# A mixture-of-experts encoder layer: the first block's token rows chosen on chip, and four smaller moves in queues and order

## Chip, cores, metric

One core of one Trainium2 chip. The metric is the device time of one execution in microseconds; the time before is the median of 3 runs.

## What is computed

All in float32, on 768 tokens of 1024 features (a prompt of 256 and a sample of 512). The two sequences meet nowhere but share all weights.

```python
h = rmsnorm(x, attn_norm)
c_q, c_kv, k_pe, dq, dk, dv = split(h @ w_in)
x = x + concat(mla(c_q, c_kv, k_pe), diff_attention(dq, dk, dv)) @ w_out
t = rmsnorm(x, ffn_norm)
g = argmax(softmax(t @ router_group + bias))                      # one of 4 groups
w2, e2 = top_k(softmax((t @ router_expert + bias)[group g]), 2)   # two of its 8 experts
out = sum over the two experts e of gate_e * (silu(t @ w_gate[e]) * (t @ w_up[e])) @ w_down[e]
y = rmsnorm(x + out, final_norm)
```

There are 32 experts with 256 inner columns: 1 MB each for gate, up and down, 3.15 MB an expert. 768 tokens make 1536 (token, expert) pairs.

## The kernel before

**Stages.** Projection and attention fill the first 388 us. Then six tiles of 128 tokens go through the out projection and the routing (388 to 486 us), then 32 experts one after another (to 775), then the combination of pairs with the residual and the last norm.

**Routing.** For each tile t VectorE adds the residual (`residual`, L1165), evacuates half of the transposed tile (L1170), computes `h2 = x * rs * gain` in one instruction (`ffn_norm`, L1176, written with the features reordered), picks group and two experts (`route`, L1193), and places the pairs in the experts' slots (`place`, L1229): TensorE's `rank` (L1608) counts the pairs of the same expert in earlier tokens, two one-hot matrices say which slot modulo 64 a token takes, and TensorE's `place` (L1622) sums, over the tiles, a table of token and pair ids for the first 64 slots of every expert. `slots` (L1247) gives the full slot number of each pair. ScalarE computes squares and root of the norm and evacuates the other half of the transposed tile. GpSimd stores h2 to HBM (L699) and scatters the pair numbers to a table of slots in HBM (`note_pairs`, L690): two scatters a tile.

**Experts.** An expert's pairs come in blocks of 64. The first block of each takes its token ids from the table in PSUM (`ids_main`); further blocks take them from the table in HBM, which the sync queue loads once (L557) and VectorE shifts into ids (`ids_further`, L1297). GpSimd gathers the rows of h2 by ids (`gather`, L713), four experts ahead, TensorE transposes them (`rows_transpose`, L1657), VectorE copies the result to `x_eT` (L1349). Gate/up is one group of 16 matmuls with the tokens stationary (`gate_up`, L1664), two 64-column halves of the array side by side; SiLU on ScalarE (L972), product on VectorE (L1326), a transpose of h (L1709), its copy (L1331), four matmuls for down (`down`, L1675), a copy by ScalarE (L980), a scatter to HBM by GpSimd (L725). 40 blocks in all, 8 of them further ones.

**Order.** All is written out by hand with semaphores, and each engine takes its instructions in program order. TensorE's order in block s is gate/up of s, transposes of the rows of s+1, down of s-1, transpose of h of s (`pe_group`, L1716). VectorE's is product of s, (ids_further, in the first block only,) copy of rows of s+1, copy of h of s (`dve_group`, L1338). The counts, which say how many further blocks an expert has, come from a chain of small VectorE instructions (L1279 to L1295) that follows the last placement; TensorE, ScalarE and GpSimd wait for them ahead of the first block.

**Weights.** Six slots for experts. The sync queue (SP) loads experts 0 to 3 at 389 us, 4 and 5 once the out projection is over (the slots hold its operands), expert 31 into the place of x, and each later expert e once the down product of e-6 is done (`load_expert`, L515, with `sp.wait_ge(last_done, e - RING + 1)`, L530); each third of an expert also waits for the third before the last issued one (L526). Between 5 and 31 that queue has

```python
store_residual(NT - 1)
sp.wait_ge(ids_scattered, 2 * NT * 16)
for h in range(2):
    sp.dma_start(yids_sb[h * SLOTS:(h + 1) * SLOTS, NE:]..., ids_dram...).then_inc(ids_loaded, 16)
sp.wait_ge(x2_stored, NT * 16)
...
load_expert(NGRP - 1, members(NGRP - 1)[-1])
```

## Time and profile before

| | us |
|---|---|
| median of 3 runs (lowest, highest) | 811.07 (810.74, 811.63) |
| the profiled execution's own time | 813.74 |
| its span, first to last instruction | 812.0 |
| TensorE busy (matmuls) | 714.7, 88% |
| VectorE, ScalarE, GpSimd busy | 322.1, 214.0, 200.9 |
| mean granted TensorE clock | 0.955 of full |
| bytes moved by DMA | 154.64 MB, mean 190 GB/s |

Times in the rows are microseconds from the start of the span. In a timeline a row has start, length, engine, line, operation, output and inputs, the count of merged instructions, and in brackets how long the engine sat idle before and what ended that. Matmuls in float32 are two instructions each; a transpose is one. In a row of windows each engine has its busy time and instruction count (TensorE's matmuls, its weight loads, VectorE, ScalarE, GpSimd), then come TensorE's granted clock, the busy share of the 16 DMA engines and GB/s. In a row of DMA queues stand packets, MB and share; q1 is the sync queue's, q0 GpSimd's. In a row of waits stand the total in us, how many, and the longest.

### The profile page before, as it was taken

The numbers are of one execution on the slowest core, as the hardware profiler recorded it, in microseconds if no ns is written. First come the engines' busy times: TensorE is split into PE (matmuls) and PEld (weight loads), VectorE is DVE, ScalarE is ACT, GpSimd is POOL, SyncE is SP. The second block draws the span as 40 slices with busy tenths as digits, with TensorE's granted clock in tenths as the row PEclk, the third lists the DMA queues.
The fourth block names the chain that finished last, engine by engine and source line by source line (L and its number), as shares of the span: only waits on it lengthen the run. The fifth ranks groups of instructions, "written<-read, shape, count | busy, mean of one in ns | idle before, by whom it ended". The sixth has DMA issues, their size and how long they took to land. (4 is left out here: it accounts for less than half of the span.)

```text
span 812.0 us, 12300 instructions
## 1 busy us (share of the span) xinstructions
PE 714.7 (88%) x3978; PEld 404.9 (50%) x3979; DVE 322.1 (40%) x900; ACT 214.0 (26%) x575; POOL 200.9 (25%) x478
## 2 busy tenths in 40 slices
PE   6899999999898999998999974999987999998810
PEld 3455544444365666664455552555544555554500
DVE  3853121110078988881545562111211221111138
ACT  2433211011167777772211110111110111110122
POOL 1224231220014230232001123441332433541110
PEclk9999999999979999999999986999999999999975
DMA  8703002000140000000792158899999999999856
GB/s 302 292 1 105 0 1 103 1 0 1 39 174 1 1 2 1 1 2 1 293 417 120 67 206 304 289 348 372 371 352 388 368 376 361 379 363 377 361 221 257
DMA packets 40824, 154.64 MB, mean 190 GB/s; under 512 B 9642, under 2 KB 10794, under 8 KB 31936
## 3 DMA queue, kind: packets, MB, share of 16 engines
q1 hardware_dynamic: 33120, 138.20, 45.5%
q0 software_dynamic: 7648, 15.75, 5.8%
q8 instruction: 28, 0.46, 0.2%
q14 instruction: 28, 0.23, 0.1%
HBM read 142.29 MB, written 20.03 MB: 200 GB/s over the span
## 5 line engine op out<-in xcount | busy, mean ns | idle before, releaser
L1405 PE MATMUL banks<-arena 128*128 128x512 f32 (+1 forms) x384 | 163.2, 579 | 9.9 <-DMA arena<-w_in 7.6
L1670 PE MATMUL banks<-arena 128*64 128x256 f32 x1280 | 151.2, 390 | 11.5 <-DMA arena<-w_up 7.4
L1670 PEld LDWEIGHTS banks<-arena 128*64 128x64 f32 x1280 | 95.0, 140 | 60.9 <-issue 18.6
L1405 PEld LDWEIGHTS banks<-arena 128*128 128x128 f32 x384 | 72.1, 193 | 85.2 <-issue 78.0
L1561 PE MATMUL banks<-arena 128*128 128x512 f32 x192 | 86.4, 598 | 1.1 <-DVE arena L1162 1.1
L1679 PE MATMUL banks<-arena 128*64 128x512 f32 x320 | 79.7, 610 | 0.5 <-ACT arena L980 0.5
L1326 DVE TENSOR_TENSOR arena<-arena,banks 128x128 f32<-128x128 f32 x40 | 11.5, 287 | 165.7 <-ACT arena L972 165.7
L1118 DVE TENSOR_REDUCE arena<-banks 128x1 f32<-128x512 f32 (+1 forms) x96 | 55.2, 598 | 52.0 <-PE banks L1477 43.9
L903 ACT ACTIVATE arena<-banks,arena 128x512 f32<-128x512 f32 (+1 forms) x96 | 58.2, 611 | 45.7 <-DVE arena L1121 22.3
L1561 PEld LDWEIGHTS banks<-arena 128*128 128x128 f32 x192 | 35.1, 190 | 38.8 <-issue 37.5
L972 ACT ACTIVATE arena<-banks 128x128 f32<-128x128 f32 x40 | 11.1, 277 | 161.3 <-PE banks L1670 161.3
L725 POOL DMA_INDIRECT pair_rows<-arena x40 | 40.4, 1010 | 35.2 <-POOL arena L723 33.1
L717 POOL DMA_INDIRECT arena<-h_rows,arena x40 | 39.1, 977 | 34.9 <-POOL arena L715 34.9
L836 ACT ACTIVATE arena<-banks,arena 128x512 f32<-128x512 f32 (+1 forms) x24 | 16.0, 666 | 113.8 <-PE banks L1405 112.8
L1512 PE MATMUL banks<-arena 128*128 128x128 f32 x240 | 36.8, 285 | 8.5 <-issue 6.4
L1477 PE MATMUL banks<-arena 96*128 96x512 f32 (+1 forms) x96 | 41.9, 562 | 2.1 <-ACT arena L903 1.2
L1660 PE MATMUL banks<-arena 64*128 64x64 f32 x320 | 28.8, 231 | 15.7 <-DMA arena<-h_rows,arena 15.7
L1512 PEld LDWEIGHTS banks<-arena 128*128 128x128 f32 x240 | 26.7, 144 | 31.0 <-issue 26.5
L463 POOL TENSOR_SCALAR arena<-arena 128x2 f32<-128x2 f32 (+1 forms) x8 | 1.5, 193 | 154.4 <-ACT arena L931 154.4
L607 POOL TENSOR_TENSOR arena<-arena 128x64 f32<-128x64 f32 (+2 forms) x24 | 7.9, 327 | 124.6 <-ACT arena L836 69.9
L980 ACT ACTIVATE arena<-banks 128x512 f32<-128x512 f32 x32 | 19.1, 597 | 71.8 <-PE banks L1679 71.8
L1660 PEld LDWEIGHTS banks<-arena 64*128 64x128 f32 x320 | 23.3, 141 | 28.9 <-issue 17.8
(179 smaller groups left out, 856.3 us busy)
## 6 DMA issues: line engine op xcount, KB each, us to landing
arena<-w_gate SPq DMA_DIRECT2D x32, 1024.0 KB, 12.8
arena<-w_up SPq DMA_DIRECT2D x32, 1024.0 KB, 13.4
arena<-w_down SPq DMA_DIRECT2D x32, 1024.0 KB, 13.1
arena<-w_in SPq DMA_DIRECT2D x3, 2048.0 KB, 8.4
arena<-pair_rows SPq DMA_DIRECT2D x5, 1024.0 KB, 11.2
arena<-w_out SPq DMA_DIRECT2D x1, 4096.0 KB, 12.9
arena<-xT SPq DMA_DIRECT2D x6, 512.0 KB, 10.3
arena<-x SPq DMA_DIRECT2D x6, 512.0 KB, 10.7
```

The lines of the kernel that those rows point to most:

```text
L717: pool.indirect_dma_start(x_rows[i], None, h2_dram, bass.IndirectOffsetOnAxis(ap=id_cur[0:SLOTS, i:i + 1], axis=0), bounds_check=T - 1, oo ...
L725: pool.indirect_dma_start(y_dram, bass.IndirectOffsetOnAxis(ap=yid_cur[:, i:i + 1], axis=0), y_sb[i], None, bounds_check=4 * T - 1, oob_is ...
L903: act.activation(p_tok[u % 3][:, a, 0:nt * P], bank(2 * (u % 2) + a)[:, 0:nt * P], ACT.Exp, bias=nbias[:, u % 4, a:a + 1], scale=MLA_SCALE ...
L980: act.activation(y_sb[s % YBUF], bank(4), ACT.Copy).then_inc(y_out, 1)
L1118: dve.reduce_max(mx[:, u % 4, a:a + 1], bank(2 * (u % 2) + a)[:, 0:nt * P], X_).then_inc(dve_chain, 1)
L1405: last = nc.tensor.matmul(bank(mm % 2)[:, 0:GROUP_COLS[g]], xgT[:, t, c, :], w[:, c, :], start=(c == 0), stop=(c == DC - 1))
L1477: nc.tensor.matmul(bank(2 * (u % 2) + a)[:, 0:nt * P], qT[0:QK, 2 * j + a, tok], kT[0:QK, 2 * j + a, keys], start=True, stop=True).then_in ...
L1512: last = nc.tensor.transpose(bank(4 + tau % 2)[:, kt * P:(kt + 1) * P], p_tok[u % 3][:, a, kt * P:(kt + 1) * P], ident)
L1561: last = nc.tensor.matmul(bank(2 * (t % 2) + h), aT[:, c, t * P:(t + 1) * P], w_out_sb[:, c, h * 512:(h + 1) * 512], start=(c == 0), stop= ...
L1660: last = nc.tensor.transpose(bank(b)[:, c * SLOTS:(c + 1) * SLOTS], x_rows[i][:, c * P:(c + 1) * P], ident[half, half])
L1670: last = nc.tensor.matmul(bank(b)[h * SLOTS:(h + 1) * SLOTS, 0:2 * P].rearrange("p (g n) -> p g n", g=2), x_eT[i][:, c, :], w[:, :, c, h * ...
L1679: last = nc.tensor.matmul(bank(4)[h * SLOTS:(h + 1) * SLOTS, :], h_T[:, j * SLOTS:(j + 1) * SLOTS], w[:, j, h * 512:(h + 1) * 512], start= ...
```

## The change

- h2 loses its gain: ScalarE writes `x * rs`, VectorE computes only the reciprocal. The gain is multiplied in where VectorE took the transposed rows out of PSUM (all 40 blocks), from a new 4 KB column load; the 512 KB broadcast of gain goes.
- The rows of expert 0's block are not gathered: VectorE weighs the one-hot slot matrices with the mask of expert 0 and the norm (`choose`), TensorE multiplies them with x, six tiles summed in bank 4 (`choose`, the two halves of the features in the two halves of the columns), ScalarE copies the sum, 16 matmuls transpose it.
- The sync queue stores the last residual tile ahead of the weights of experts 4 and 5. Before expert 31 it waits no longer for the scatters of ids; it waits for the last selection instead.
- The table of further ids is loaded on ScalarE's queue, after the first SiLU. VectorE's `ids_further` moves behind the copies of the first block.
- VectorE's count chain moves behind the multiply for expert 0; TensorE waits for the counts after the first gate/up. The first down product comes ahead of the second gate/up.
- On chip memory is laid out anew for this; the counts move from bank 1 to bank 2.

```diff
@@ sync queue
+                    sp.dma_start(gain_rows, A["ffn_norm"].rearrange("o (p c) -> (o p) c", c=DC)).then_inc(lam_loaded, 16)
...
-            sp.dma_start(gain_ffn, A["ffn_norm"].to_broadcast([P, D])).then_inc(gffn_in, 16)
...
             sp.wait_ge(oproj, 2 * NT)
+            store_residual(NT - 1)
             load_expert(0, 4)
             load_expert(0, 5)
-            store_residual(NT - 1)
-            sp.wait_ge(ids_scattered, 2 * NT * 16)
-            for h in range(2):
-                sp.dma_start(yids_sb[h * SLOTS:(h + 1) * SLOTS, NE:].rearrange("r (b e) -> r b e", e=NE),
-                             ids_dram.rearrange("(b r e) o -> r b (e o)", b=NBLK, e=NE)[:, 1:, :]).then_inc(ids_loaded, 16)
             sp.wait_ge(x2_stored, NT * 16)
             sp.wait_ge(h2_ready, NT)
             sp.wait_ge(rms2_ready, NT)
             sp.wait_ge(x2T_psum, 2 * NT)
+            sp.wait_ge(chosen_psum, 1)
             load_expert(NGRP - 1, members(NGRP - 1)[-1])
@@ GpSimd
-            gather_main(0, 0)
+            pool.sem_inc(id_ready, 1)
             gather_main(0, 1)
             note_pairs(NT - 1)
@@ ScalarE
+            def ffn_norm(t):
+
+                act.wait_ge(norm_ready, t + 1)
+                if t >= 2:
+                    act.wait_ge(h2_stored[t % 2], 16 * (t // 2))
+                act.activation(h2[t % 2].rearrange("n (c p) -> n c p", c=DC), x_tok[:, t, :].rearrange("n (p c) -> n c p", c=DC),
+                               ACT.Copy, scale=rs[:, t:t + 1]).then_inc(h2_ready, 1)
...
+            act.wait_ge(chosen_psum, 1)
+            act.activation(x_sel, bank(4), ACT.Copy).then_inc(chosen_rows, 1)
             act.wait_ge(gates_in, 1)
             act.activation(gate_in, gate_in, ACT.Exp).then_inc(gates_exp, 1)
...
+            def load_further_ids():
+
+                act.wait_ge(ids_scattered, 2 * NT * 16)
+                for h in range(2):
+                    act.dma_start(yids_sb[h * SLOTS:(h + 1) * SLOTS, NE:].rearrange("r (b e) -> r b e", e=NE),
+                                  ids_dram.rearrange("(b r e) o -> r b (e o)", b=NBLK, e=NE)[:, 1:, :]).then_inc(ids_loaded, 16)
...
                     silu(e + before)
+                    if isinstance(g, int) and e == 0:
+                        load_further_ids()
@@ VectorE
+            def choose(t):
+
+                for i, mask in enumerate((m1_all, m2_all)):
+                    dve.tensor_scalar(share[:, i:i + 1], mask[:, t, 0:1], rs[:, t:t + 1], None, ALU.mult).then_inc(dve_chain, 1)
+                    chain[0] += 1
+                dve.wait_ge(dve_chain, chain[0])
+                dve.wait_ge(onehot_ready, 2 * t + 2)
+                link(dve.tensor_scalar(select[:, t, :], onehot[:, 0, 0:SLOTS], share[:, 0:1], None, ALU.mult))
+                dve.scalar_tensor_tensor(select[:, t, :], onehot[:, 1, 0:SLOTS], share[:, 1:2], select[:, t, :],
+                                         ALU.mult, ALU.add).then_inc(select_ready, 1)
...
             slots(NT - 1)
+            dve.wait_ge(xeT_psum, 1)
+            dve.tensor_tensor(x_eT[0], bank(0).rearrange("p (c n) -> p c n", c=DC), gain_eT, ALU.mult).then_inc(xeT_ready, 1)
 
             dve.wait_ge(counts_psum, 1)
...
                     h_product(k)
+                    if not isinstance(g, int) or e + 1 < NE:
+                        dve.wait_ge(xeT_psum, e + 2)
+                        dve.tensor_tensor(x_eT[(s + 1) % 2], bank(0).rearrange("p (c n) -> p c n", c=DC), gain_eT, ALU.mult).then_inc(xeT_ready, 1)
+                    hT_evac(k)
                     if isinstance(g, int) and e == 0:
                         ids_further()
-                    if not isinstance(g, int) or e + 1 < NE:
-                        dve.wait_ge(xeT_psum, e + 2)
-                        dve.tensor_copy(x_eT[(s + 1) % 2], bank(0).rearrange("p (c n) -> p c n", c=DC)).then_inc(xeT_ready, 1)
-                    hT_evac(k)
@@ TensorE
+            def choose(t):
+
+                pe.wait_ge(select_ready, t + 1)
+                for h in range(2):
+                    last = nc.tensor.matmul(bank(4)[h * SLOTS:(h + 1) * SLOTS, :], select[:, t, :],
+                                            x_tok[:, t, h * 512:(h + 1) * 512], start=(t == 0), stop=(t == NT - 1))
+                return last
...
             router(NT - 1, 1)
+            for t in range(3):
+                choose(t)
             rank(NT - 1)
+            choose(3)
+            place(NT - 1)
+            choose(4)
+            choose(5).then_inc(chosen_psum, 1)
...
-            place(NT - 1)
...
+                    early = first and s == 1
...
+                    if early:
+                        down_weights(g, 0)
+                        down_before(k, g, 0, last_done)
                     pe.wait_ge(xeT_ready, e + 1)
                     gate_up(1, s % 2, weights(g, s)).then_inc(gu_done, 1)
                     if not isinstance(g, int) or e + 1 < NE:
                         transpose_rows(g, s + 1)
-                    if not isinstance(g, int) or e:
+                    if first and s == 0:
+                        pe.wait_ge(counts_ready, 1)
+                        words = load_counts(pe, g)
...
+                    elif not early:
                         down_weights(g, s - 1)
                         down_before(k, g, s - 1, last_done)
...
-            pe.wait_ge(rows_in[0], 16)
-            rows_transpose(0, 0, range(DC)).then_inc(xeT_psum, 1)
-            pe.wait_ge(counts_ready, 1)
+            pe.wait_ge(chosen_rows, 1)
+            x_sel_c = x_sel.rearrange("n (p c) -> n c p", c=DC)
+            for c in range(DC):
+                for h in range(2):
+                    half = slice(h * SLOTS, (h + 1) * SLOTS)
+                    last = nc.tensor.matmul(bank(0)[half, c * SLOTS:(c + 1) * SLOTS], x_sel_c[half, c, :], ident[half, half],
+                                            start=True, stop=True)
+            last.then_inc(xeT_psum, 1)
             pe_group(0)
```

## Rows read from the trace of the kernel before

**Rows 1.** Windows: us, busy us by engine, clock, DMA share, GB/s.

```profile
476.50:496.50 20.00, 6.05 (x36) 5.53 (x35) 10.52 (x45) 2.60 (x6) 8.48 (x11) 0.57 0.99 382
496.50:500.50 4.00, 2.69 (x16) 2.04 (x18) 0.86 (x3) 0.29 (x2) 2.23 (x5) 0.50 0.25 47
500.50:510.50 10.00, 8.91 (x69) 5.89 (x66) 1.73 (x5) 1.56 (x3) 1.72 (x4) 0.87 1.01 333
510.50:514.50 4.00, 4.00 (x31) 2.00 (x32) 1.27 (x3) 0.81 (x2) 2.30 (x4) 1.00 0.45 112
600.00:640.00 40.00, 34.58 (x259) 18.94 (x257) 7.04 (x16) 4.37 (x10) 11.32 (x20) 0.96 1.02 373
```

**Rows 2.** Timeline of TensorE: start us, us, instruction, idle before.

```profile
476.84 2.03 PE L1603 MATMUL banks<-arena 128*128 128x36 f32 x16
...
485.50 1.09 PE L1627 MATMUL banks<-arena 128*128 128x64 f32 x4
496.93 1.11 PE L1660 MATMUL banks<-arena 64*128 64x64 f32 x8 [10.34 <-DMA arena<-h_rows,arena]
498.92 5.75 PE L1670 MATMUL banks<-arena 128*64 128x256 f32 x32 [0.88 <-DVE arena L1358]
...
506.73 3.67 PE L1670 MATMUL banks<-arena 128*64 128x256 f32 x32 [1.05 <-DVE arena L1349]
...
510.98 1.94 PE L1679 MATMUL banks<-arena 128*64 128x512 f32 x8
...
513.10 3.67 PE L1670 MATMUL banks<-arena 128*64 128x256 f32 x32
```

**Rows 3.** Timeline of the sync queue (SP).

```profile
498.07 1.32 SPq L557 DMA_DIRECT2D arena<-pair_of_slot  x2
...
513.36 0.35 SPq L534 DMA_DIRECT2D arena<-w_gate  x1
...
519.64 0.33 SPq L534 DMA_DIRECT2D arena<-w_gate  x1
```

**Rows 4.** Waits of TensorE from 513, and of SP from 470.

```profile
PE banks L1670 <- DMA arena<-w_up: 7.4, 5, 2.5
...
SPq L531 <- PE banks L1679: 20.6, 5, 11.7
```

**Rows 5.** Timeline of VectorE.

```profile
475.61 0.69 DVE L1168 TENSOR_TENSOR arena<-arena,banks 128x512 f32<-128x512 f32 x1 [1.48 <-PE banks L1561]
477.04 0.69 DVE L1174 COPY arena<-banks 128x512 f32<-128x512 f32 x1 [0.75 <-PE banks L1592]
...
478.12 2.06 DVE L1184 SCALAR_TENSOR_TENSOR arena<-arena 128x1024 f32<-128x1024 f32 x1
...
487.43 0.18 DVE L1279 COPY arena<-banks 1x32 f32<-1x32 f32 x1
...
489.95 0.16 DVE L1294 CAST arena<-arena 1x12 int32<-1x12 f32 x1
...
505.01 0.29 DVE L1326 TENSOR_TENSOR arena<-arena,banks 128x128 f32<-128x128 f32 x1 [6.07 <-ACT arena L972]
...
505.58 0.40 DVE L1304 TENSOR_SCALAR arena<-arena 128x352 uint32<-128x352 uint32 x1
```

**Rows 6.** Timeline of ScalarE.

```profile
498.97 0.23 ACT L964 ACTIVATE arena<-arena 128x30 f32<-128x30 f32 x1 [19.79 <-DVE arena L1311]
500.44 1.28 ACT L972 ACT_TABLE_LOAD   x1 [1.23 <-issue]
```

**Rows 7.** DMA queues: two from 488.6 to 490.6, q1 from 499.9 to 501.

```profile
q1 hardware_dynamic: 113, 0.79, 94.1%
q0 software_dynamic: 105, 0.03, 6.6%
...
q1 hardware_dynamic: 1123, 0.16, 99.7%
```

**Rows 8.** DMA queue q1 from 514 to 528.5.

```profile
q1 hardware_dynamic: 644, 3.83, 79.1%
```

More of the change, by code:

```diff
@@ L222, in build @@
         gain_in = k.take(DC)
+        gain_rows = k.take(DC)
         gains = k.take(4)
@@ L275, in build @@
         macc = m.take(NT * NE).rearrange("p (t e) -> p t e", t=NT)
-        bias_r = m.take(NG + NE)
-        ones = m.take(P)
-        logit = m.take(NT * (NG + NE)).rearrange("p (t e) -> p t e", t=NT)
-        top = m.take(1)
-        max_g, max_1, max_2 = (m.take(NT) for _ in range(3))
-        rank_f = m.take(2)
-        onehot = m.take(2 * P).rearrange("p (i n) -> p i n", i=2)
-        slot_of = m.take(4 * NE).rearrange("p (i w e) -> p i w e", i=2, w=2)
         r_g = m.take(3 * NG)
@@ L286, in build @@
         slot_f = m.take(2)
-        junk_c = m.take(256).bitcast(bf16)
+        rank_f = m.take(2)
+        bias_r = m.take(NG + NE)
+        top = m.take(1)
+        max_g, max_1, max_2 = (m.take(NT) for _ in range(3))
+        share = m.take(2)
         cnt = m.take(NE)
@@ L291, in build @@
         pk = m.take(NGRP * RING)
+        logit = m.take(NT * (NG + NE)).rearrange("p (t e) -> p t e", t=NT)
         m = Area(WORDS - DC * (NG + NE) - DC, WORDS)
@@ L1261, in _ @@
                 x2T_evac(t)
-                ffn_norm(t)
+                norm(t)
                 route(t)
@@ L1355, in dve_group @@
                             hT_evac(k + j + 1)
-            dve.wait_ge(xeT_psum, 1)
-            dve.tensor_copy(x_eT[0], bank(0).rearrange("p (c n) -> p c n", c=DC)).then_inc(xeT_ready, 1)
             gate_inputs()
@@ L1648, in _ @@
             router(NT - 1, 1)
+            for t in range(3):
+                choose(t)
             rank(NT - 1)
-            counts = bank(1)[:, 0:NE]
+            choose(3)
+            place(NT - 1)
+            choose(4)
+            choose(5).then_inc(chosen_psum, 1)
+            counts = bank(2)[:, 0:NE]
             nc.tensor.matmul(counts, ones, macc[:, NT - 2, :], start=True, stop=False)
@@ L1716, in pe_group @@
             def pe_group(g):
-                words = load_counts(pe, g)
+                first = isinstance(g, int) and g == 0
+                if not first:
+                    words = load_counts(pe, g)
                 for s in members(g):
                     e = g * RING + s
-                    n, before = extras(words, s)
-                    k = e + before
                     if is_last(g, s):
@@ L1726, in pe_group @@
                         pe.wait_ge(up_loaded[s], 16 * (g + 1))
+                    early = first and s == 1
+                    if not first or s:
+                        n, before = extras(words, s)
+                        k = e + before
+                    if early:
+                        down_weights(g, 0)
+                        down_before(k, g, 0, last_done)
                     pe.wait_ge(xeT_ready, e + 1)
```

41 lines of the change are left out of this document (24 added, 17 removed).

## Prediction, made before the changed kernel was run

> **What bounds the kernel now.** I read the stretch totals first, then each engine in order of time, then who waited for whom. [Rows 1] cut the switch from routing to experts into stretches. From 476.5 to 496.5 the DMA engines are full (share 0.99) with the weights of experts 4 and 5. Then they are nearly empty to 500.5 (0.25), full while expert 31 loads, half empty from 510.5 to 514.5 (0.45), and full again until the last weights (1.02 in the row of 600 to 640, 373 GB/s). TensorE's granted clock is 0.57 and then 0.50, its lower level of 1.2 GHz. [Rows 2] show why: its last routing work starts at 485.50, the gathered rows of expert 0 let it go on at 496.93 after 10.3 idle us, the first gate/up product starts at 498.92, the second at 506.73, and the first down product at 510.98. [Rows 3] show the sync queue behind that: it waits until 498.07 for the scatters of ids, loads the ids, issues expert 31 only then, and expert 6 at 513.36, after that down product; expert 7 follows at 519.64, behind the down product of expert 1. Later TensorE loses only 7.4 us to weights, in five waits of at most 2.5 [rows 4]. The sync queue waits for down products five times, 20.6 us in total, the first 11.7 [rows 4]. So from 514 on the weight stream, 25 experts long, sets the end, and TensorE has a few us of slack. What counts is how much sooner the stream runs without holes.
>
> **The change, part by part.** *Normalization.* The fused norm and gain leaves VectorE (2.06 us, starting 478.12) and a scaled copy goes to ScalarE. For tiles 0 to 4 both lie beside the out projection, which keeps TensorE back to back. In the last tile the logits are done at 476.84 + 2.03 = 478.87, so routing starts at 478.95 and not at the norm's end, 478.12 + 2.06, about 480.1 [rows 2, 5]: 1.1 us earlier. The selection weights add four small VectorE operations a tile, under 1 us, less than what leaves: nothing. The multiply by gain that takes the place of a 128x512 copy reads a bank as the residual add of that shape does, 0.69 us, and so long is the copy too [rows 5]: nothing.
>
> *Selection.* A down product is 4 matmuls in 1.94 us [rows 2] with the same shapes as two selections, so one selection is 0.97 us. Three fit where TensorE idles now, and so does the fourth. The last placement would start at 485.5 - 1.1 = 484.4, takes 0.56, and two more selections follow: 486.9. ScalarE copies (0.60), then 16 matmuls transpose. In instructions that is 32, each between 0.069 us (8 transposes in 1.11 at half clock, halved) and 0.127 (16 logit instructions in 2.03) [rows 2]: 2.2 to 4.1 us; I take 3.4, nearer to the logits, whose instructions also load new weights each time. VectorE adds 0.69, the start 0.15. The first gate/up starts at 491.7, not 498.92: 7.2 us earlier.
>
> *First block.* The count chain, 2.7 us [rows 5], now stands behind the first gain multiply: counts at 494.3. ScalarE then needs 2.75 us from the gate exponential to the end of its table load [rows 6], so SiLU is done near 497.6 and the product at 497.9, later than gate/up itself. Rows of expert 1 are the first gather of GpSimd's queue, issued where expert 0's was, which let TensorE go on at 496.93 [rows 2], so they come about 497 to 498, and their transposed copy is ready at 499.4. The first down product is now ahead of the second gate/up: 499.7 to 501.7. The second gate/up starts at 501.7 (5.0 earlier), and expert 6 is issued at 502 instead of 513.36.
>
> *Weight stream.* Expert 31 is issued near 487, when 4 and 5 still occupy the engines. The holes go: 4.0 x 0.75 + 4.0 x 0.55 = 5.2 us. The last residual store ahead of the weights delays them: that add ends at 475.61 + 0.69 = 476.30 [rows 5], where today the weights go as soon as TensorE is through, near 475.5, and the store's issue comes on top in part: 0.9. One gather less is about 0.15 MB, 0.4 us. Without any new stall the stream is 5.2 - 0.9 + 0.4 = 4.7 us earlier. At the start of the kernel one more small load stands ahead of the third tile's x in the sync queue. An issue there takes up to 0.66 us (two in 1.32 [rows 3]); hidden if the first tiles' work covers it, passed on in full if not: 0 to 0.66, I take 0.4 later. The 512 KB broadcast of gain that goes was hidden in a stretch where experts 0 to 3 load long before use: nothing.
>
> *The ids of further blocks, now on ScalarE's queue.* This decides. They are two loads of 704 runs of 128 bytes. 1123 packets of the sync queue move 0.16 MB in 1.1 us [rows 7], so each run is a packet: 88 for each of 16 engines. Today they go when that queue holds nothing else, and VectorE finds them landed right behind its first product, at 505.3 [rows 5]. In the change they go near 499 (the scatters of ids stand behind the gather in GpSimd's queue, and ScalarE first does SiLU), while the sync queue holds expert 31 and then 6. How two queues share an engine is in [rows 7]: between 488.6 and 490.6 GpSimd's queue has 105 packets for 0.03 MB, the sync queue 113 for 0.79 MB. They alternate one for one, whatever the size. That is 113/16 = 7.1 turns in 2 us, 0.283 us a turn; 88 turns need 25 us. No row has a load on ScalarE's queue; the nearest are GpSimd's.
> The Trainium skill says otherwise for the size of a turn (DMA: Bandwidth & Descriptors, section Queues, rings and completion order): an engine drains a whole packet, typically 9 to 17 descriptors, before it switches. By that, 88 descriptors are 5 to 10 turns, some 3 us, and the 4.7 us would be kept; it is a rival below.
>
> By the rows, the sync queue has work until: 476.5 + 0.9 + 20 - 0.4 = 497.0, expert 31 with gathers 9.0, expert 6 with gathers 9.5, so 515.5. Until then 15.7/0.283 = 55 of 88 turns are done; the rest run alone in 1 us: landed at 516.5. VectorE waits for them **ahead of expert 1's product**, which would be ready at 505.7. Behind it stand the copy of expert 2's rows, TensorE's transpose of h, gate/up of expert 2, and the down product of expert 1, for which the sync queue waits before expert 7. VectorE needs 0.7 for the ids (505.3 to 505.98) and 0.29 for the product [rows 5], then the copy: gate/up of expert 2 starts at 518.6, not 513.10 [rows 2]. After 12 idle us TensorE is at half clock, as it was for the product at 498.92: 5.75 us instead of 3.67 [rows 2], 2.1 more. Transposes (1.11 at half clock, halved) and the down product of expert 1 take 0.6 + 1.94 more, to 526.9, and expert 7 is issued at 527.3 instead of 519.64, its data from 528.6.
> The stream has then nothing from 515.5 to 528.6. Today the sync queue moves 3.83 MB from 514 to 528.5 [rows 8]; expert 6 is 3.15 of them, so 0.68 MB of expert 7 and about one gather and one scatter (0.35) are ahead of the new kernel: 1.03/0.368 = **2.8 us later**. TensorE is 7.6 us later at expert 2, but its five waits for weights, 7.4 us [rows 4], absorb that, so the stream sets the end: +2.8, +0.4 at the start = **+3.2**. On the profiled execution: span 812.0 to 815.2. That execution took 813.74, the median of the runs is 811.07, 2.7 less, and I carry the difference over: 814.3.
>
> **Rivals.** (a) *The ids land in time.* If a turn takes many small packets, or ScalarE's loads share the sync queue's order, or the sync queue runs dry before expert 6 is issued (that needs the first down product 3.5 us later than I have it, and then 1 us empties the ids), VectorE's wait is 0 to 2 us. For: the product at 505.7 has 6 us after their issue, and today, issued from 498.07 on, they are there by 505.3 at the latest. Against: the one-for-one rows. Time: 811.07 - 4.7 + 0.4 = 806.8. The point from which it decides is ids landed at 505.
> (b) *A draw.* The stall is there, but the ids end sooner (turns against 4 KB packets are shorter) or the half clock is avoided: then expert 7 comes 3 us earlier, its lag of 2.8 is gone: 811.5.
> (c) *TensorE carries its delay to the end.* At most one wait, 2.5 us of the 7.6, is absorbed, because the sync queue then waits for slots and the stream slips with TensorE: 811.07 + 5.1 + 0.4 = 816.6. For: five waits for down products exist already. Against: only the first is long.
> (d) *The rows chosen on chip don't come early*, because ScalarE or the gather of expert 1 holds the second block at 506 as now: then the first block moves nothing, but the stream still gains its holes: 807 to 809 if the ids are in time.
>
> **How the numbers follow.** Forecast 814.3, chance 0.62. Rival (a) 0.23, (d) 0.03, (b) 0.07, (c) 0.05. About 0.2% (1.6 us) is what can be told from no change here. The forecast's own range is 812.0 to 816.5, of which a tenth lies within 0.2%. Faster: 0.23 + 0.03 and a little: 0.27. Same: 0.07 + 0.06 = 0.13. Slower: 0.60. The range must reach to (a) and lean to (c): 806.3 to 817.0. Its middle is unlikely; the two cases stand apart.
>
> **What would show it.** Right: two loads of pair_of_slot by ScalarE of 12 us or more to landing; VectorE's shift of ids starting near 516; TensorE idle some 12 us before gate/up of expert 2, at half clock behind; DMA share near 0 from 516 to 528; the first gate/up near 491.7 and expert 6's issue near 502. Wrong: ids shifted before 508 with expert 2's gate/up near 506 and no hole in the DMA row; then the time is below 808. If the hole is there and the time is still lower, my count of the stream is wrong.

## The result: 0.9% slower, and the profile after

The changed kernel took 819.76 us (median of 4 runs, 816.40 to 821.52) beside 811.35 us for the kernel before (4 runs, 810.74 to 812.97): ratio 1.0091, 95% interval [1.0067, 1.0115]. (The ratios here are estimates from all runs; the quotient of these two medians is 1.0104.) It is slower, as forecast, but by 8.4 us and not by 3.2, and 819.76 lies outside the range of 806.3 to 817.0. The profiled execution took 816.40 (span 814.6), the fastest of the four.

In that execution the last router product starts at 474.26 and not at 476.84 [rows 2]. The edit touches little ahead of it, and in the other profiles below that date lies anywhere from 473.70 to 478.91. So two kernels are compared by the time since that product ("since the logits"), and only differences of that are read. The timeline of TensorE in the changed kernel (start, duration, line and form, idle time before it and what ended it):

```profile
474.26 2.03 PE L1633 MATMUL banks<-arena 128*128 128x36 f32 x16
...
484.83 2.14 PE L1809 MATMUL banks<-arena 64*64 64x64 f32 x32
487.92 6.65 PE L1713 MATMUL banks<-arena 128*64 128x256 f32 x32 [0.95 <-DVE arena L1308]
...
497.40 3.72 PE L1722 MATMUL banks<-arena 128*64 128x512 f32 x8 [0.59 <-DVE arena L1363]
500.83 3.74 PE L1713 MATMUL banks<-arena 128*64 128x256 f32 x32
...
516.84 0.48 PE L1752 MATMUL banks<-arena 128*128 128x128 f32 x1 [11.63 <-DVE arena L1358]
517.53 5.51 PE L1713 MATMUL banks<-arena 128*64 128x256 f32 x32 [0.21 <-DVE arena L1379]
```

The first half is the plan of the change, and it works: first gate/up at 487.92, second at 500.83, with the down product of expert 0 ahead of it. Then TensorE is idle for 11.63 us on VectorE, and gate/up of expert 2 starts at the lower clock: 5.51 us instead of 3.67. Since the logits it starts at 43.27, in the kernel before at 36.26 [rows 2]: 7.0 later. VectorE, the queue of ScalarE and the sync queue of the same kernel say why:

```profile
515.70 0.34 DVE L1333 TENSOR_SCALAR arena<-arena 64x352 uint32<-64x352 uint32 x1 [18.56 <-DMA arena<-pair_of_slot]
516.07 0.40 DVE L1336 TENSOR_SCALAR arena<-arena 128x352 uint32<-128x352 uint32 x1
516.50 0.29 DVE L1358 TENSOR_TENSOR arena<-arena,banks 128x128 f32<-128x128 f32 x1
```
```profile
496.51 1.36 ACTq L1008 DMA_DIRECT2D arena<-pair_of_slot  x2
```
```profile
484.22 0.33 SPq L540 DMA_DIRECT2D arena<-w_gate  x1
...
501.56 0.35 SPq L540 DMA_DIRECT2D arena<-w_gate  x1
...
525.89 0.33 SPq L540 DMA_DIRECT2D arena<-w_gate  x1
```

The ids are issued at 496.51 and are not there until 515.7, 19 us later; in the kernel before, VectorE shifted them right behind its first product of 505.01, without a wait [rows 5]. Expert 31 is issued at 484.22, expert 6 at 501.56 and expert 7 at 525.89: since the logits, 6 is 9.2 us earlier than in the kernel before and 7 is 8.8 later [rows 3]. How the ids travelled is read from the DMA queues (packets, MB, share; q1 is the sync queue, q10 ScalarE's). Of their 1440 packets, 1408 of them runs of 128 bytes, none starts in the 4.9 us behind the issue. First the stretch from 501.4 to 504, then that from 504 to 506:

```profile
q1 hardware_dynamic: 222, 0.93, 92.2%
q10 hardware_dynamic: 224, 0.03, 7.5%
```
```profile
q1 hardware_dynamic: 94, 0.39, 75.5%
q10 hardware_dynamic: 952, 0.12, 52.6%
```

In the first the two queues take turns one for one: 14 turns on each of the 16 DMA engines in 2.6 us, 0.19 us a turn. In the second the sync queue has little to move, between the weights of expert 31 and those of expert 6, and two thirds of the ids pass. The other 264 packets need until 515.2, beside the weights of expert 6, and VectorE waits for the last of them. By windows, the DMA engines fall empty at 514 (the columns are the window, its length, busy time of PE, PEld, DVE, ACT and POOL, granted clock, DMA share, GB/s):

```profile
508.00:512.00 4.00, 0.00 (x0) 0.00 (x0) 0.00 (x0) 0.00 (x0) 0.00 (x0) 0.50 1.01 401
...
514.00:516.00 2.00, 0.00 (x0) 0.00 (x0) 0.30 (x1) 0.00 (x0) 0.00 (x0) 0.50 0.10 32
516.00:518.00 2.00, 0.95 (x4) 0.52 (x6) 1.59 (x5) 0.00 (x0) 0.00 (x0) 0.50 0.00 0
...
520.00:526.00 6.00, 6.00 (x41) 3.12 (x39) 1.13 (x3) 0.68 (x2) 3.06 (x7) 0.89 0.26 72
```

How far behind is the stream? The DMA queues from the logits to 52 us behind them, first the kernel before (476.84 to 528.84), then the changed one (474.26 to 526.26); q0 is GpSimd's:

```profile
q1 hardware_dynamic: 3906, 13.96, 74.3%
q0 software_dynamic: 1217, 2.23, 13.7%
```
```profile
q1 hardware_dynamic: 2384, 13.11, 69.0%
q0 software_dynamic: 808, 1.37, 8.5%
q10 hardware_dynamic: 1440, 0.18, 2.8%
```

With the 0.18 MB of ids counted in, the sync queue's work is 0.67 MB behind, where the forecast had 0.68. GpSimd's is 0.86 MB behind, where it had 0.35. GpSimd's row of that stretch says why: it waits for the same shifted ids ahead of all its further gathers, those of main rows too, and stands still for 23.16 us.

```profile
518.28 0.18 POOL L718 COPY arena<-arena 64x1 uint32<-64x1 uint32 x1 [23.16 <-issue]
```

Later, who waited for whom in the changed kernel, TensorE's rows from 510 on, and then the sync queue's from 470 on; against [rows 4] the waits for weights fell from 7.4 to 3.6 us, and the sync queue's waits for down products rose from 20.6 (5 times) to 66.5 (10 times):

```profile
PE banks L1703 <- DMA arena<-h_rows,arena: 5.0, 3, 3.8
PE banks L1713 <- DMA arena<-w_up: 3.6, 3, 1.6
```
```profile
SPq L537 <- PE banks L1722: 66.5, 10, 22.1
```

### The profile page after: what moved, and what is told of

Read it like the earlier page. It is cut to its first block and busy times, and to the rows that moved or that the text cites. A ratio compares the mean times of both kernels' runs of the same rounds, so it can differ in the third digit from the quotient of the medians.

```text
span 814.6 us, 12425 instructions
## 1 busy us (share of the span) xinstructions
PE 721.7 (89%) x4026; PEld 406.1 (50%) x4027; DVE 315.0 (39%) x918; ACT 227.3 (28%) x582; POOL 199.7 (25%) x476
## 3 DMA queue, kind: packets, MB, share of 16 engines
q10 hardware_dynamic: 1440, 0.18, 0.2%
## 5 line engine op out<-in xcount | busy, mean ns | idle before, releaser
L1713 PE MATMUL banks<-arena 128*64 128x256 f32 x1280 | 153.2, 394 | 8.2 <-DMA arena<-w_up 3.6
L1713 PEld LDWEIGHTS banks<-arena 128*64 128x64 f32 x1280 | 96.0, 142 | 59.7 <-issue 17.4
L1722 PE MATMUL banks<-arena 128*64 128x512 f32 x320 | 81.5, 621 | 1.1 <-DVE arena L1363 0.6
L1591 PEld LDWEIGHTS banks<-arena 128*128 128x128 f32 x192 | 35.1, 190 | 38.8 <-issue 37.5
L1507 PE MATMUL banks<-arena 96*128 96x512 f32 (+1 forms) x96 | 40.0, 539 | 2.1 <-ACT arena L906 1.2
L1121 DVE COPY arena<-banks 128x512 f32<-128x512 f32 x12 | 8.3, 689 | 65.3 <-PE banks L1481 65.3
L1722 PEld LDWEIGHTS banks<-arena 128*64 128x64 f32 x320 | 20.8, 139 | 23.6 <-issue 18.4
## 6 DMA issues: line engine op xcount, KB each, us to landing
arena<-w_up SPq DMA_DIRECT2D x32, 1024.0 KB, 12.8
arena<-w_down SPq DMA_DIRECT2D x32, 1024.0 KB, 13.7
```

The costliest lines, as they stand in the source:

```text
L1507: nc.tensor.matmul(bank(2 * (u % 2) + a)[:, 0:nt * P], qT[0:QK, 2 * j + a, tok], kT[0:QK, 2 * j + a, keys], start=True, stop=True).then_in ...
L1591: last = nc.tensor.matmul(bank(2 * (t % 2) + h), aT[:, c, t * P:(t + 1) * P], w_out_sb[:, c, h * 512:(h + 1) * 512], start=(c == 0), stop= ...
L1713: last = nc.tensor.matmul(bank(b)[h * SLOTS:(h + 1) * SLOTS, 0:2 * P].rearrange("p (g n) -> p g n", g=2), x_eT[i][:, c, :], w[:, :, c, h * ...
L1722: last = nc.tensor.matmul(bank(4)[h * SLOTS:(h + 1) * SLOTS, :], h_T[:, j * SLOTS:(j + 1) * SLOTS], w[:, j, h * 512:(h + 1) * 512], start= ...
```

## The experiments

Each kernel was run 4 to 12 times and is set against the kernel before, run on the same chip beside it. They came in four groups, with medians of the kernel before of 812.87 (the first four kernels), 812.75 (the next four), 812.34 (the next four) and 812.48 us (the last two). TensorE computes 40 blocks of rows, expert by expert: a main block each, and eight further ones at experts 8, 9, 13 (three), 14, 15 and 19.

**The changed kernel again** (no edit).

> The changed kernel once more, for a second trace and the spread of its times. Theory (ids on ScalarE's queue take one turn each against weights, VectorE, GpSimd and TensorE wait behind them): VectorE's shift of ids again near 515 to 518, a hole of 11 to 14 us in the DMA engines, 6 to 10 us slower than before in the median. Rival (the loss is in this one execution, or lies elsewhere): the ids land at another time, and the time moves with something else.

819.18 us (816.84 to 821.59), ratio 1.0076 [1.0057, 1.0094]. Since the logits, gate/up of expert 2 starts at 43.30, as in the first trace (43.27), and the ids are shifted at 41.5 (41.4); the wait for them is 18.9 us. But they travelled otherwise: 474 of their packets had started by 510, 31.1 since the logits, where the first trace had 1176 by 31.7, and the rest went on in turns to the end (99 packets of each queue from 510 to 512, 0.32 us a turn, with 7.5 KB in a packet of weights). So the same date was reached in two ways.

**The ids back on the sync queue, behind expert 31:**

```diff
             load_expert(NGRP - 1, members(NGRP - 1)[-1])
+            sp.wait_ge(ids_scattered, 2 * NT * 16)
+            for h in range(2):
+                sp.dma_start(yids_sb[...], ids_dram...).then_inc(ids_loaded, 16)
...
                     silu(e + before)
-                    if isinstance(g, int) and e == 0:
-                        load_further_ids()
```

> Only the two loads of ids go back to the sync queue, now behind expert 31's weights and ahead of expert 6's. Theory: in one queue they need no turns, they land behind expert 31, near 504 to 507, VectorE waits 0 to 2 us, the hole in the DMA engines is gone, and the kernel is 3.5 to 5.5 us faster than before (about 806 to 808). Rival (the loss is the chosen rows, the early down product or the store ahead of the weights): the time stays above 815.

812.74 us, ratio 1.0003 [0.9988, 1.0018]: the loss is gone, the 3.5 to 5.5 us of gain that I expected are not there. In one queue the ids stand behind the weights of expert 31 and take no turns with those of expert 6: shifted 12.8 us after their issue and not 19.2, but VectorE still waits 12.0 us, where I expected 0 to 2.

**ScalarE's queue, but only blocks 1 to 3 of 11** (24 runs of 128 bytes an engine and not 88; enough for these inputs, where no expert has more than three further blocks):

```diff
-  act.dma_start(yids_sb[..., NE:]..., ids_dram...[:, 1:, :])
+  act.dma_start(yids_sb[..., NE:4 * NE]..., ids_dram...[:, 1:4, :])
```

> Still on ScalarE's queue, but only the ids of further blocks 1 to 3 of 11: 24 runs of 128 bytes for each DMA engine, not 88 (no expert of this input has more blocks; the rest of the table is not loaded). Theory, one turn a run at 0.28 us: 6.8 us to landing plus 1 to 2, so VectorE's shift near 505 to 507 and the time at or below before's, 805 to 809. Rival, a turn takes 9 to 17 runs: then 88 runs would be 5 to 10 turns and 24 runs 2 to 3, both few us, and the landing hardly changes with the number. Rival, the wait is for the scatters of ids: the shift stays near 515.

811.08 us, ratio 0.9981 [0.9965, 0.9997]: shifted 12.1 us after issue, VectorE waits 11.3. The first packet starts 4.8 us after the issue, which the expected 8 to 9 us left out. Since the logits, the third gate/up starts at 36.8 with the ids on the sync queue and at 36.1 with three blocks, beside 43.3 in the changed kernel and 36.3 in the kernel before. So the loss of the change hangs on the landing of the ids, and that, on ScalarE's queue, on the number of their runs.

**GpSimd waits for the ids only where it gathers a further block:**

```diff
-            pool.wait_ge(ids_ready, 3)
+            pool.wait_ge(ids_ready, 2)
...
                     with pool.If(n > 0):
+                        pool.wait_ge(ids_ready, 3)
                         await_count(e_xeT_psum, before + 1)
```

> The changed kernel, but GpSimd waits for the shifted ids only where an expert has a further block, no longer ahead of the gather of expert 4. Theory (what my sum left out: GpSimd's gathers of experts 4 to 7 and the first scatter stood behind the ids as well and came on top of the weights later): gathers 4 to 6 are issued before 505, the hole in the DMA engines is as long, and the time is 1.5 to 2.5 us below the changed kernel's. Rival (TensorE's delay alone sets the loss): no difference beyond 0.5 us.

821.58 us, ratio 1.0109 [1.0086, 1.0132], where I expected 1.5 to 2.5 us less than the changed kernel's: the gathers now take turns as well, and the ids land still later (VectorE of this kernel):

```profile
522.77 0.34 DVE L1334 TENSOR_SCALAR arena<-arena 64x352 uint32<-64x352 uint32 x1 [23.69 <-DMA arena<-pair_of_slot]
```

So letting GpSimd go on in those 23 us won nothing: what its gathers gained, the ids lost.

At this point I held that TensorE's date is the bound up to expert 15 and that a delay of it is passed on in full but for the one wait of 1.75 us ahead of expert 13. The next runs were made to test that, and it fell.

**The kernel before, with more work for TensorE alone:** the gate/up products of experts 3 and 4 computed twice.

```diff
+                    if isinstance(g, int) and g == 0 and s in (3, 4):
+                        gate_up(1, s % 2, weights(g, s))
                     gate_up(1, s % 2, weights(g, s)).then_inc(gu_done, 1)
```

> The kernel before, in which TensorE computes the gate/up product of expert 3 and of expert 4 twice (two times 3.67 us more, the same values written again), and nothing else is touched. These products stand behind the issue of expert 7 and well ahead of the one wait for weights before expert 13 (1.75 us). Theory of the forecast (the weight stream sets the end, TensorE's five waits for weights absorb 7.4 us): no change, ratio 0.998 to 1.002. Theory now (TensorE carries a delay through to the expert at which the slots are full, where the load of expert 21 waits for the last product of expert 15, and only the wait of 1.75 us before expert 13 is absorbed): +5.6 us, ratio 1.0069, with expert 21 issued 5 to 6 us later against the last logits and in a burst of three loads.

813.95 us, ratio 1.0016 [0.9996, 1.0036]: 1.2 us for 7.3 us of work, and the interval still includes no change. The +5.6 us of my theory is refuted; "no change", by the theory of the forecast, is nearly right here. At expert 16 TensorE is 6.9 us late all the same, so the rest goes later, at expert 27. TensorE of the kernel before waits there for weights and then starts a product at the lower clock (2.53 + 5.36 - 3.67 = 4.2 us lost); with the extra work it does neither (first the kernel before, then this one):

```profile
737.50 5.36 PE L1670 MATMUL banks<-arena 128*64 128x256 f32 x32 [2.53 <-DMA arena<-w_up]
```
```profile
738.82 3.67 PE L1670 MATMUL banks<-arena 128*64 128x256 f32 x32
```

**The ids on ScalarE's queue, VectorE shifts them at expert 3 and not at expert 0** (right only where the first further block comes later, as here; GpSimd's wait as above):

```diff
-                    if isinstance(g, int) and e == 0:
+                    if isinstance(g, int) and e == 3:
                         ids_further()
```

> The changed kernel with its ids on ScalarE's queue, but VectorE shifts them only at expert 3, and GpSimd waits for them only where it gathers a further block (the first is at expert 8, so this holds for these inputs). The loads run as slowly as before and nobody waits for them. Theory (the wait alone costs the time, the turns do not): no idle of 11 us before the third gate/up, which starts near 506.5 if the logits are where they were, some 6 us earlier than in the kernel before; TensorE's gain is carried through to the end: -4 to -7 us against before, ratio 0.991 to 0.995. Rival A (the slow turns themselves hold back the weights or the gathers, so that rows of experts 2 and 3 come late): the third gate/up earlier, but idle on rows behind it, -1 to +2 us. Rival B (the stream sets the end once TensorE is early): the gain stops at about 2 to 3 us, with longer waits for weights at experts 7 to 13 than the 1.75 us of before.

814.87 us, ratio 1.0029 [1.0013, 1.0045], where I expected -4 to -7 us. It did not take the wait away: with weights and gathers in the other queues the ids, issued at 496.0, are shifted at 533.6, VectorE waits 14.2 us for them at expert 3, and TensorE 9.6.

**The same on the sync queue behind expert 31**, and **this with the first down product back behind the second gate/up** (`early = False`):

> As the kernel in which nobody waits for the ids, but the two loads go out on the sync queue behind expert 31, ahead of expert 6. Theory: within 1.5 us of the one with ScalarE's queue, somewhat later because the wait for the second of two issues holds expert 6 back by about 2.9 us: -3 to -6 us against before. Rival (ScalarE's queue also costs something by its turns): 1 us or more better than that one.

811.34 us, ratio 0.9987 [0.9965, 1.0009]: 3.5 us below the one on ScalarE's queue, so the rival was right. Against the kernel before it is 1.4 below, where I expected 3 to 6.

> As the kernel with the loads on the sync queue and nobody waiting, but the first down product stays behind the second gate/up. If moving it up matters: expert 6 is issued about 5.7 us later (a gate/up and a down product), a hole of that size stands in the weight stream, the second gate/up is up to 1.9 us earlier, and the third unchanged. Theory (TensorE is the bound up to expert 15, the stream has slack there): within 1.5 us of it with the down product moved up. Rival (the stream sets the end): 4 to 5 us slower than that.

810.87 us, ratio 0.9977 [0.9960, 0.9994]: where the ids don't wait in turns, the place of the down product makes no difference that can be told. In both, the third gate/up is 4 to 5 us earlier since the logits, and that is lost in the main at expert 13 (TensorE of the first of the two; the kernel before had 1.75 and 3.67 there):

```profile
597.62 6.63 PE L1716 MATMUL banks<-arena 128*64 128x256 f32 x32 [5.75 <-DMA arena<-w_up]
```

**The extra work at half and at double dose:** the product of expert 3 twice (+3.67 us), and those of 3 and 4 three times (+14.7 us). The theory is now one of two bounds.

> The kernel before with the gate/up product of expert 3 computed twice: +3.67 us of TensorE and nothing else. Theory of two bounds: the end is the later of two dates, that of the weight stream and that of TensorE at the last product of expert 15, which lets the load of expert 21 go; in the kernel before TensorE has 1.75 us of slack ahead of expert 13 and some 4.3 behind it (the idle ahead of the 36th block in the list of TensorE's blocks), about 6 in all. Then 3.67 us cost nothing: ratio 0.9985 to 1.0015. Rival (TensorE carries its delay to the end but for 1.75 us): +1.9 us, ratio 1.0024.

811.36 us, ratio 0.9993 [0.9977, 1.0010]: nothing, as expected.

> The same with the products of experts 3 and 4 computed three times each: +14.7 us of TensorE. Two bounds: 14.7 - 6.1 = +8.6 us, ratio 1.0106, with the last product of expert 15 some 14 us later against the last logits and the wait for weights behind it gone. Rival (one slope, as 7.3 us cost 1.2): +2.4 us, ratio 1.003. Rival (carried but for 1.75 us): +12.9 us, ratio 1.016.

822.83 us, ratio 1.0131 [1.0107, 1.0154]: +10.5 us against 8.6 expected (1.0106, just below the interval). 3.7 us cost nothing, 7.3 cost 1.2 and 14.7 cost 10.5: a knee, no slope.

**Three blocks on ScalarE's queue, shifted at expert 3:**

> The changed kernel with only blocks 1 to 3 of the ids loaded on ScalarE's queue (24 runs an engine), and VectorE shifting them at expert 3, GpSimd waiting for them only ahead of a further gather. The ids are landed near 510, so nobody waits. Two bounds: the weight stream has no hole at the switch, the third gate/up is 4 to 5 us earlier against the last logits than in the kernel before, but TensorE then stalls 4 to 6 us for the weights of expert 13 and runs that product at the lower clock, and a hole of 4 to 6 us stands in the stream where experts 19 to 21 wait for slots: -1 to -3 us, ratio 0.9965 to 0.999. Rival (without ids in the way the gain of the switch is kept): -5 us, ratio 0.994.

806.95 us (804.79 to 807.92), ratio 0.9929 [0.9907, 0.9950]. The rival of this run was right: the gain of the switch is kept, and ahead of expert 13 there is almost no stall:

```profile
590.87 3.67 PE L1714 MATMUL banks<-arena 128*64 128x256 f32 x32 [0.33 <-DMA arena<-w_up]
```

**The changed kernel with nothing but the first down product put back** (`early = False`):

> The changed kernel, its ids on ScalarE's queue as they are, with the first down product behind the second gate/up. Expert 6 is then issued 2 to 4 us later, which expert 31's data (until about 505) covers: the ids still take turns with weights all the way. Theory: within 1 us of the changed kernel (ratio 1.007 to 1.010), ids landed 15 to 18 us after issue. Rival (a) of the forecast (the sync queue runs dry ahead of expert 6, the ids then land at once): ids landed 4 or more us earlier, and the time 4 us below the changed kernel's.

810.80 us, ratio 0.9984 [0.9962, 1.0005]: 9.0 us below the changed kernel's median (against the kernel before of their own groups: -1.5 beside +8.4 and +6.3). I had expected no difference; the rival was right. Its sync queue and VectorE:

```profile
506.73 0.35 SPq L540 DMA_DIRECT2D arena<-w_gate  x1
```
```profile
509.49 0.34 DVE L1333 TENSOR_SCALAR arena<-arena 64x352 uint32<-64x352 uint32 x1 [10.91 <-DMA arena<-pair_of_slot]
```

Since the logits, expert 6 is issued 3.6 us later (30.9 and not 27.3). The sync queue is again short of weights for a moment, from 506 to 508, and 1027 packets of the ids pass. But now the last 122 pass before the weights of expert 6 fill the engines, and the ids, issued at 497.64, are shifted at 509.5. The third gate/up starts at 35.5.

**All blocks on ScalarE's queue, down product in its place, shifted at expert 3:**

> The changed kernel with all 11 blocks of ids on ScalarE's queue, the first down product behind the second gate/up (so that expert 6 does not stand in the ids' way), VectorE shifting them at expert 3 and GpSimd waiting for them only ahead of a further gather. Theory: the ids are landed by 513 and nobody waits; the third gate/up is about 5 us earlier against the last logits than in the kernel before, and the gain of the switch is kept as in the run with three blocks: -4 to -6 us, ratio 0.9925 to 0.995, with TensorE at the last product of expert 15 earlier than in the kernel before. Rival (it was the number of runs of ids that cost the two kernels with the loads on the sync queue their gain): -1 to -2 us, with a stall of over 4 us for the weights of expert 13.

809.76 us, ratio 0.9964 [0.9938, 0.9989], half of what was expected. The free gathers again took turns, the ids were not there before 525.5, and VectorE waited 4.7 us:

```profile
525.55 0.34 DVE L1334 TENSOR_SCALAR arena<-arena 64x352 uint32<-64x352 uint32 x1 [4.73 <-DMA arena<-pair_of_slot]
```

**Three blocks on the sync queue, shifted at expert 3** (4 runs):

> The changed kernel with blocks 1 to 3 of the ids loaded on the sync queue behind expert 31, nobody waiting. If the place on the sync queue is what cost the kernel with all blocks there its gain: as that one, ratio 0.998 to 1.000 and a stall of over 4 us for expert 13's weights. If it was the number of runs: as the run with three blocks on ScalarE's queue, ratio 0.991 to 0.995, stall below 3 us.

806.87 us (806.00 to 807.91), ratio 0.9937 [0.9920, 0.9955]. With three blocks the queue makes no difference (with all of them it did: 814.87 and 811.34); the number of runs separates the kernels that kept the gain from those that didn't. From 20 to 40 us since the logits, by windows, the kernel with all blocks on the sync queue moves 304 GB/s, this one 335, with the engines busy in both:

```profile
494.57:514.57 20.00, 16.47 (x119) 11.22 (x121) 3.43 (x8) 1.64 (x4) 7.72 (x14) 0.91 1.07 304
```
```profile
494.40:514.40 20.00, 17.42 (x125) 11.52 (x127) 3.43 (x8) 1.64 (x4) 7.90 (x15) 0.91 1.04 335
```

That is 0.62 MB, 1.7 us of weights. By 130 us since the logits the sync queue has moved 38.49 MB and 39.71, a gap of 1.2 MB or 3.3 us; the two medians are 4.5 us apart. Why the gap goes on growing after the ids have landed is not settled. One more thing differs: the kernel with all blocks takes 4.76 us to issue the ids and 4.90 to issue the gate weights of expert 6, this one 1.28 and 0.35. With the down product in its place the two take 2.30 and 0.35, and the time is no better (810.87), so that can't be the main part.

## Where the time went, by three dates

The dates are those of TensorE's transpose of h behind the gate/up product of expert 5, of expert 16 (next to the last product of expert 15, which frees the slot of expert 21's weights) and of expert 31, each since the logits. In the kernel before they are 61.5, 185.7 and 295.8 us. The rows of the second date, first the kernel before (662.54 - 476.84 = 185.7), then the changed one (669.07 - 474.26 = 194.8), and with each the sync queue's loads of expert 21:

```profile
662.54 0.33 PE L1709 MATMUL banks<-arena 128*128 128x128 f32 x1
```
```profile
662.95 0.33 SPq L534 DMA_DIRECT2D arena<-w_gate  x1
664.82 0.33 SPq L534 DMA_DIRECT2D arena<-w_up  x1
668.42 0.38 SPq L538 DMA_DIRECT2D arena<-w_down  x1
```
```profile
669.07 0.33 PE L1752 MATMUL banks<-arena 128*128 128x128 f32 x1
```
```profile
669.48 0.33 SPq L540 DMA_DIRECT2D arena<-w_gate  x1
669.99 0.33 SPq L540 DMA_DIRECT2D arena<-w_up  x1
670.50 0.38 SPq L544 DMA_DIRECT2D arena<-w_down  x1
```

In the kernel before the three loads come 2 and 4 us apart, at the queue's own pace; in the changed one at once, because the queue had nothing left and waited for the slot. Later (+) or earlier (-) than in the kernel before, in us:

| kernel | expert 5 | expert 16 | expert 31 | medians |
|---|---|---|---|---|
| changed | +8.8 | +9.1 | +5.2 | +8.4 |
| changed, again | +9.0 | +9.6 | +5.8 | +6.3 |
| ids on the sync queue | +2.4 | +2.9 | -1.0 | -0.1 |
| three blocks | +1.6 | +1.9 | -2.0 | -1.8 |
| gathers free | +15.0 | +13.3 | +9.5 | +8.7 |
| one product more | +3.7 | +2.8 | -1.0 | -1.0 |
| two more | +7.1 | +6.9 | +2.0 | +1.2 |
| four more | +13.5 | +12.0 | +6.7 | +10.5 |
| shifted at 3, ScalarE's queue | +7.2 | +6.7 | +3.5 | +2.1 |
| shifted at 3, sync queue | -4.0 | +5.7 | +0.7 | -1.4 |
| the same, down in place | -5.3 | +6.3 | +1.4 | -1.9 |
| changed, down in place | +1.2 | +1.4 | -2.4 | -1.5 |
| all blocks, down in place, shifted at 3 | -4.8 | -1.6 | -2.2 | -2.7 |
| three blocks, shifted at 3 | -4.5 | -4.1 | -3.9 | -5.4 |
| three on the sync queue, shifted at 3 | -4.5 | -3.8 | -5.4 | -5.6 |

The first three columns are one profile each (one product more, which can't be faster than the kernel before, ends 1.0 earlier: so far may a single one be off), the last is the difference of medians. The rows read together: **wherever expert 16 is later than before, the end is later by 3.2 to 5.3 us less than that** (3.8 or 3.9 in seven of the twelve, the changed kernel among them). That is the slack which TensorE has in the kernel before between expert 16 and the end; it stands there as the wait and the slow product at expert 27, 4.2 us. Where expert 16 is not later, I take it that the weight stream sets the end. Then the end is the later of two dates: that of the stream, and that of TensorE at the slot of expert 21. The doses bear out the knee; which of the two dates is the later one in the changed kernel is read from its profile and was not tested by a run of its own.

## Why the prediction was wrong, point by point

- **Routing, selection, first block: right in direction.** Since the logits, the first gate/up came at 13.7 and not at 22.1: 8.4 earlier, forecast 7.2. The 32 transposes took 2.14 us, just under the lower end of my bound (2.2), not 3.4. The second gate/up came only 3.3 earlier (5.0 forecast), because the down product ahead of it ran at the lower clock, 3.72 us where I had 2.0. So expert 6 was issued at 27.3, forecast 25.2.
- **The norm copy.** I said it lies beside other work, and so it does, but it takes ScalarE 2.16 us, as long as VectorE took for norm and gain together (2.06 [rows 5]).
- **The ids in turns: right in kind, close in part by luck.** Landed 41.4 us since the logits, forecast 39.7. One packet a turn held in both traces. But I had counted from the issue, and the first packet came 4.9 us later; a turn took 0.19 us beside packets of 4 KB and 0.32 beside those of 7.5 KB, where I had 0.283 throughout; and I had no gap between experts 31 and 6, in which 952 of the 1440 packets passed in 2 us. These misses nearly cancelled. The Trainium skill's rule of 9 to 17 descriptors a turn (DMA: Bandwidth & Descriptors, section Queues, rings and completion order) does not hold here: a turn of ScalarE's queue was one packet of 128 bytes; from 501.4 to 502.0 the two queues moved 47 and 48 packets, three for each engine. (The 3 us that I worked out from it also took a turn of the weights' queue to be one packet, which that rule doesn't give.) Rival (a) did not come about: the sync queue did run short, but after expert 6 was issued, and the ids were shifted 41.4 us since the logits and not 28.
- **The stall: right.** TensorE idle 11.6 us (12 forecast), the product at 5.51 us, the DMA engines empty from 39.7 since the logits (38.7), expert 7 issued at 51.6 (50.5).
- **The stream term: under-sized.** I wrote "0.68 MB of expert 7 and about one gather and one scatter (0.35)", 2.8 us. Measured 0.67 and 0.86 MB: (0.67 + 0.86) / 0.368 = 4.2 us. What I had missed is that GpSimd's whole loop stands behind the wait for the shifted ids. With that the sum would have been 4.2 + 0.4 = +4.6, inside the range.
- **The step that failed:** "TensorE is 7.6 us later at expert 2, but its five waits for weights, 7.4 us, absorb that, so the stream sets the end". TensorE was 7.0 later at the start of that product and 8.8 behind it (the 7.6 of the forecast), still 9.1 at expert 16, and only 3.9 were absorbed from there on: +5.2. Its waits for weights did fall, by 7.4 - 3.6 = 3.8, and could fall no further, since the loads now waited for TensorE (66.5 us and not 20.6). The total of the waits was not the slack: the wait before expert 13 absorbed 1.75, most of which the further blocks of expert 13 took back (from the second of its blocks to the third 13.1 us in the changed kernel, 11.7 before). The dose of 7.3 us says how large the slack is in the kernel before: 4.9 us of it were absorbed by the profiles, 6.1 by the medians, less than 7.4 and more than the 2.5 of rival (c). So this is the mechanism of rival (c), which I gave 0.05 and 5.1 us, with more slack than it had and a later TensorE. The stream, with its term put right, comes within 1 us of it. The argument against it, "only the first is long", read the sync queue's waits in a kernel where TensorE was early, and they say nothing of one where it is late.
- **The rest, 0.5 to 3.2 us between +5.2 or +5.8 in the profiles and +6.3 or +8.4 in the medians,** is not settled. The small load at the start (0.4 forecast) may be in it; it was not tried alone, and the starts of the profiles vary by more than that.
- **Which part did it.** The first down product moved up, alone: 819.8 with it, 810.8 without. It sends expert 6 in between the ids and their landing: 264 packets of ids were left when its weights came. The forecast had this as a condition of rival (a), "the sync queue runs dry before expert 6 is issued (that needs the first down product 3.5 us later than I have it)", and did not see that one part of the change decides it.

Two versions beat both kernels: 806.95 and 806.87 us, 0.6 to 0.7% below the kernel before. Both load 3 of 11 blocks and shift them at expert 3, so they hold only for inputs with at most three further blocks for an expert and none ahead of expert 3. The kernel that loads all blocks (the first down product put back, shift at expert 3) gains 0.4%, with none ahead of expert 3 either.

## What to carry to other kernels

On this evidence a load of many small runs has a price in turns, one run a turn against every other queue with work; what is issued between its start and its landing sets how long it takes, so moving a large load earlier can delay a small one on which an engine waits. Find the slack of an engine at the one place where the others wait for it, not from the sum of its waits; putting some idle work on it, at two or three doses, shows the knee. Where an engine waits for something that is needed only later, move the wait to the first use.

## What the runs showed of the hardware that I had not expected

- Three queues share the engines one for one too: with GpSimd's gathers free, 152 packets of the sync queue, 149 of GpSimd's and 136 of ScalarE's started from 514 to 518. The two loads were there 46.6 us since the logits and not 41.4, and with the shift at expert 3 as well they took 37.5 us from issue to the shift.
- The first packet of the ids on ScalarE's queue started 4.9 us after the issue in both traces of the changed kernel and 4.8 in those with three blocks and with the down product in place. In the kernel before, on the sync queue, it was 1.7. What makes the difference no run shows.
- The same 128-byte runs inside one queue, behind expert 31, went with a slower stream: 304 against 335 GB/s over 20 us for 88 and 24 runs an engine.
- A scaled copy of a 128x1024 tile on ScalarE, its columns read eight apart, takes 2.16 us; the plain copy of half a tile from a bank takes 0.60. How much of that is the stride was not tried:

```profile
475.53 2.16 ACT L962 ACTIVATE arena<-arena 128x1024 f32<-128x1024 f32 x1 [0.23 <-DVE arena L1203]
...
484.16 0.60 ACT L976 ACTIVATE arena<-banks 128x512 f32<-128x512 f32 x1 [6.48 <-PE banks L1665]
```
